# The last up projection by seven block products, with GpSimd forming the weight and token sums

## The chip, the cores and the metric

The kernel runs on one core of a Trainium2 chip. The metric is the device time in microseconds from the first to the last instruction of one execution, as the median of several runs. The core's engines run side by side, each in the order of its own instructions: TensorE (PE in the rows; its weight loads are PEld), VectorE (DVE), ScalarE (ACT), GpSimd (POOL) and the DMA queues (SP's issues most of them here). They meet through semaphores. TensorE's granted clock was 1.00 of full speed (2.4 GHz, the higher of its two levels) over the whole execution before.

## What is computed

The reference runs two transformer-like blocks over 512 tokens of width 1024. What the change touches is the very last feed-forward part, `swiglu` on the normalised and modulated stream `y`:

```python
def swiglu(y, w_in, w_out):
    a, b = jnp.split(y @ w_in, 2, axis=-1)
    return (jax.nn.silu(a) * b) @ w_out
...
D_FF = 2816
...
x = ada_out(x, swiglu(ada_in(x, mod, 2, norm_pre[l, 2]), ffn_w_in[l, 1], ffn_w_out[l, 1]),
            mod, 2, norm_post[l, 2], 0.5)
```

`y @ w_in` is the up projection, 512 x 1024 by 1024 x 5632. Its 5632 columns are 44 tiles of 128; tile j (of `a`) and tile 22 + j (of `b`) make one pair, 22 pairs in all. `@ w_out` is the down projection, 512 x 2816 by 2816 x 1024.

## The kernel before

**Numbers in two parts.** Matmuls take fp32 numbers as a high part (rounded to the matmul's format) and a low part (the rest). `mm3` makes one product of them by three matmuls: high by high, high by low, low by high (lines 540 to 542 in the profile). Activations of 1024 x 512 live in HH and HL (8 blocks of 128 x 512 each), hidden values in GH and GL.

**Weights.** They stream from HBM in chunks of 128 x 1024 fp32 (eight blocks of 128 x 128, so one tile of 128 output columns over the whole depth of 1024). SP issues the loads in order into the ring `stage` of 4 slots; a slot is loaded again once the chunk in it has been split. ScalarE copies a chunk to WH (line 1708) and VectorE subtracts to get WL (line 2569). WH and WL are rings of 3 chunks: a chunk can be split once TensorE has finished the one three before it. TensorE waits for `wlo` of its chunk.

**The last feed-forward part** (`swiglu("y", 1, half, ...)`, half 0 and half 1). Each half does 11 pairs: tile "sa" (8 blocks, 24 matmuls of 512 columns), tile "sb" (24 more), each in a bank of PSUM from a ring of 6. ScalarE applies silu to "sa" (line 2129) into SCR, VectorE multiplies "sb" onto it (line 3182), ScalarE writes the high part to GH (`hidden`, line 1728) and VectorE the low part to GL (`hidden_low`, line 2611). Then eight tiles "sd" of the down projection run over the 11 hidden blocks of this half, and the second half is added. The first pair and "sa" of the second are entwined with the norm ahead of them. GpSimd has nothing to do in this part until the closing norm. X, Z, TAB, CB and MST are tensors in SBUF that earlier stages used; CB and MST (128 x 2 x 1024 each) and TAB (128 x 2048) are idle by then.

**What sets the order.** Every engine's program is written out by hand, in the same loops; `weights(name, ahead)` on ScalarE and VectorE splits the chunks that the named tile needs, and some ahead.

Of the kernel before, what the change touches and what calls it, by code (L numbers as in the profile page):

```python
# [12 lines left out]
S = 512  # L13
# [198 lines left out]
def program(nc, ws, wm, xT, cT, params, cond, consts, max_rows, out, plan):  # L212
# [3 lines left out]
    with ctx:  # L216
# [101 lines left out]
        def hx(k, n=S):  # L318
            return HH[:, k, 0:n], HL[:, k, 0:n]
# [93 lines left out]
        EARLY_GROUPS = [("n2", 0), ("n1", 1), ("n2", 1), ("an", 2, 0)]  # L413

        def operands(i):
            q = early_up(i)
            if q is None:
                return WH[:, i % NW, :], WL[:, i % NW, :]
            a = (12 + 2 * q) * S
            return GHf[:, a:a + 1024], GLf[:, a:a + 1024]  # L420

        def operands_free(i):

            if early_up(i) is not None:
# [91 lines left out]
        def tensor(e):  # L516
# [3 lines left out]
            def block(*specs):  # L520
                if cur["used"] + len(specs) > 8:
                    cur["n"] += 1
                    cur["used"] = 0
                    if dry:
                        chunks.append([])
# [617 lines left out]
            def ending():  # L1143
# [25 lines left out]
                plus(3, 1)  # L1169

            def swiglu(who, f, half, n, mov, ready):
# [509 lines left out]
        def scalar(e):  # L1681
# [3 lines left out]
            def weights(name=None, ahead=AHEAD):  # L1685

                want = -1 if name is None else upto.get(name, -1)
                while at["w"] <= min(want + ahead, len(chunks) - 1):
                    i = at["w"]
                    src, wh, _ = low_stage(i)  # L1690
                    if split_done(i)[0] is wlo and chunks[i][0][0] == "poolm":
# [412 lines left out]
            def closing_norm():  # L2104
# [8 lines left out]
                yield from ada_norm(0, 0, S, hx)  # L2113

            def swiglu(who, f, half, n, zt):
                def hidden(jj):
# [3 lines left out]

                for jj in range(11):
                    pair = jj == 0 and half == 0
# [7 lines left out]
                    if not pair:  # L2130
                        weights(("sb", who, half, jj))
                        walk.tick()
                hidden(10)
                if (who, half) == ("c", 1):
                    walk.pace = (1, 1)
                for nn in range(8):
# [7 lines left out]
                    if who == "y" and half and nn == 7:  # L2144
                        break
                    act.wait_ge(mm, "sd", who, half, nn)
                    if half == 0:
# [391 lines left out]
        def vector(e):  # L2539
# [3 lines left out]
            def weights(name=None, ahead=AHEAD):  # L2543

                want = -1 if name is None else upto.get(name, -1)
                while at["w"] <= min(want + ahead, len(chunks) - 1):
                    i = at["w"]
                    src, wh, wl = low_stage(i)
                    of = folded_weights(i)
# [594 lines left out]
            def closing_norm():  # L3144
# [13 lines left out]
                yield from ada_norm(0, 0, S, xx, hx)  # L3158

            def swiglu(who, f, half, n, zt):  # L3160
                def hidden_low(jj):
# [9 lines left out]

                for jj in range(11):
                    pair = jj == 0 and half == 0
# [7 lines left out]
                    dve.wait_ge(ev, "sa", who, half, jj)  # L3181
                    made(e.tensor_tensor(T, bank("sb", who, half, jj)[:, 0:n], T, ALU.mult), "sb", who, half, jj)  # L3182
                if n == S:
                    hidden_low(10)
# [3 lines left out]
                for nn in range(8):  # L3188
                    step("sd", who, half, nn)
                    if who == "y" and half and nn == 7:  # L3190
                        break
# [455 lines left out]
        def gpsimd(e):  # L3647
# [180 lines left out]
            half_root(k2, 1)  # L3828

            def end_root(s):  # L3830
# [21 lines left out]
        def sync(e):  # L3852
# [9 lines left out]
            def load(i):  # L3862
                if i >= NS:
                    sp.wait_ge(*split_done(i - NS))
# [255 lines left out]
```

## Time and profile before

| | us |
|---|---|
| median of 3 runs | 2936.25 |
| lowest, highest | 2935.87, 2936.34 |
| the profiled execution | 2936.28 |
| its span, first to last instruction | 2934.7 |
| TensorE busy | 2923.9 |
| VectorE busy | 1783.2 |
| ScalarE busy | 1128.4 |
| GpSimd busy | 238.3 |

The profiled execution is 1.6 us longer than its span and 0.03 us from the median. Busy times come from one execution. Matmuls are pipelined, so the distance from one matmul's start to the next, not its duration, says what it costs. An engine's busy time says nothing of the end unless something waits for it.

### The profile page before, as it was taken

Reading aid. Unit: us, or ns where it says so; the run is one execution under the profiler, and the core shown is the slowest. Engines: PE = TensorE matmul, PEld = TensorE weight load, DVE = VectorE, ACT = ScalarE, POOL = GpSimd, SP = SyncE. Lnnn points to the kernel's source line nnn. Section 1 sums busy time; section 2 is a strip of 40 time slices with the busy share of each in tenths; the row PEclk is TensorE's granted clock in tenths of the full one; section 3 lists DMA queues with packets and bytes.
Section 4 is the critical chain, followed back from the end, with each engine's and each line's share of the span. In section 5 each row is a group of like instructions: output and inputs, shape, how many; then the busy total and the mean of one; then the engine's idle time right before and its main releaser. Section 6 shows DMA issues by size and latency. Waiting matters only on the chain.

```text
span 2934.7 us, 36398 instructions
## 1 busy us (share of the span) xinstructions
PE 2923.9 (100%) x14793; PEld 2485.4 (85%) x14793; DVE 1783.2 (61%) x2639; ACT 1128.4 (38%) x1731; POOL 238.3 (8%) x202
## 2 busy tenths in 40 slices
PE   9999999999999999999999999999999999999999
PEld 8988888888888888888888899888889887888887
DVE  7867666865767776778856656332348667542234
ACT  4432333433534333324433345222225457432222
POOL 0300100000001200100000011000002006100001
PEclk9999999999999999999999999999999999999999
DMA  7444455334433432344434435222234340222221
GB/s 306 159 172 149 150 172 186 139 138 141 136 136 115 156 124 100 125 146 138 157 132 148 137 129 173 101 93 101 93 108 173 116 144 30 72 87 100 94 97 69
DMA packets 109334, 384.75 MB, mean 131 GB/s; under 512 B 12136, under 2 KB 15720, under 8 KB 109168
## 3 DMA queue, kind: packets, MB, share of 16 engines
q1 hardware_dynamic: 84528, 295.31, 28.6%
q10 hardware_dynamic: 24640, 87.12, 8.6%
q8 instruction: 117, 1.92, 0.3%
q14 instruction: 49, 0.40, 0.0%
HBM read 380.27 MB, written 2.11 MB: 130 GB/s over the span
## 4 chain that ended last, share of the span: by engine, by line
PE 98%; ACT 1%; POOL 0%; DVE 0%; issue 0%; DMA 0%; POOLq 0%; SPq 0%; DVEq 0%; ACTq 0%
PE ps L540 30%; PE ps L541 30%; PE ps L542 30%; PE ps L755 1%; PE ps L770 1%; PE ps L756 1%; PE ps L669 1%; PE ps L606 0%; PE ps L607 0%; PE ps L610 0%; PE ps L643 0%; POOL GL L3678 0%; DMA X<-xT 0%; PE ps L1373 0%; PE ps L1372 0%
## 5 line engine op out<-in xcount | busy, mean ns | idle before, releaser
L2569 DVE TENSOR_TENSOR WL<-stage,WH 128x1024 fp32r<-128x1024 f32 x496 | 614.0, 1239 | 552.4 <-ACT WH L1708 551.8
L540 PE MATMUL ps<-HH,WH 128*128 128x512 f32 x2152 | 839.7, 390 | 0.1
L541 PE MATMUL ps<-HL,WH 128*128 128x512 f32 x2152 | 836.2, 389 | 0.0
L542 PE MATMUL ps<-HH,WL 128*128 128x512 f32 x2152 | 835.9, 388 | 0.0
L1708 ACT ACTIVATE WH<-stage 128x1024 fp32r<-128x1024 f32 x499 | 524.1, 1053 | 429.6 <-PE ps L542 422.1
L540 PE MATMUL ps<-GH,WH 128*128 128x512 f32 (+2 forms) x1678 | 574.4, 342 | 0.0
L541 PE MATMUL ps<-GL,WH 128*128 128x512 f32 (+2 forms) x1678 | 572.6, 341 | 0.0
L542 PE MATMUL ps<-GH,WL 128*128 128x512 f32 (+2 forms) x1678 | 572.6, 341 | 0.0
L542 PEld LDWEIGHTS ps<-HH,WL 128*128 128x128 f32 x2152 | 404.1, 188 | 84.1
L540 PEld LDWEIGHTS ps<-HH,WH 128*128 128x128 f32 x2152 | 404.3, 188 | 81.9 <-issue 1.1
L541 PEld LDWEIGHTS ps<-HL,WH 128*128 128x128 f32 x2152 | 404.3, 188 | 80.1
L540 PEld LDWEIGHTS ps<-GH,WH 128*128 128x128 f32 x1678 | 317.8, 189 | 38.3
L541 PEld LDWEIGHTS ps<-GL,WH 128*128 128x128 f32 x1678 | 317.9, 189 | 37.6
L542 PEld LDWEIGHTS ps<-GH,WL 128*128 128x128 f32 x1678 | 317.8, 189 | 35.9
L1728 ACT ACTIVATE GH<-SCR 128x512 fp32r<-128x512 f32 (+5 forms) x310 | 165.9, 548 | 420.1 <-DVE SCR L2907 125.2
L2596 DVE CUSTOM_DVE_ANT_0 MST<-MST,CB,PAR 128x1024 f32<-128x1024 f32 x158 | 205.2, 1299 | 2.3 <-DMA MST<-wm 1.8
L2611 DVE TENSOR_TENSOR GL<-SCR,GH 128x512 fp32r<-128x512 f32 (+1 forms) x192 | 124.3, 656 | 58.8 <-ACT GH L1728 57.2
L3678 POOL TENSOR_TENSOR GL<-SCR,GH 128x512 fp32r<-128x512 f32 (+3 forms) x102 | 121.8, 1212 | 412.0 <-ACT GH L1728 411.6
L2026 ACT ACTIVATE SCR<-ps,PAR 128x512 f32<-128x512 f32 x88 | 68.0, 775 | 153.2 <-PE ps L542 138.3
L3182 DVE TENSOR_TENSOR SCR<-ps,SCR 128x512 f32<-128x512 f32 (+1 forms) x66 | 39.7, 602 | 122.1 <-PE ps L542 110.8
L3656 POOL TENSOR_TENSOR V<-V,HM 128x4 f32<-128x4 f32 (+1 forms) x20 | 25.7, 1285 | 1033.2 <-DVE V L2639 1033.2
L2129 ACT ACTIVATE SCR<-ps 128x512 f32<-128x512 f32 (+1 forms) x66 | 34.7, 525 | 185.6 <-PE ps L542 178.8
(333 smaller groups left out, 2920.6 us busy)
## 6 DMA issues: line engine op xcount, KB each, us to landing
stage<-ws SPq DMA_DIRECT2D x533, 512.0 KB, 3.3
MST<-wm ACTq DMA_DIRECT2D x154, 512.0 KB, 3.3
Z<-wm SPq DMA_DIRECT2D x10, 512.0 KB, 8.9
TAB<-consts ACTq DMA_DIRECT2D x7, 448.0 KB, 3.5
MST<-wm SPq DMA_DIRECT2D x6, 512.0 KB, 9.0
Z<-max_rows ACTq DMA_DIRECT2D x8, 256.0 KB, 4.3
out<-X SPq DMA_DIRECT2D x16, 128.0 KB, 1.8
X<-xT SPq DMA_DIRECT2D x2, 512.0 KB, 6.1
```

The lines of the kernel that those rows point to most:

```text
L540: e.matmul(o, wh, mh, start=start, stop=False, **more)
L541: e.matmul(o, wh, ml, start=False, stop=False, **more)
L542: return e.matmul(o, wl, mh, start=False, stop=stop, **more)
L1708: e.activation(wh, src, ACT.Copy).then_inc(whi.sem, whi.up(("w", i)))
L1728: e.activation(dst, src, ACT.Identity if "bias" in more else ACT.Copy, **more).then_inc(hi.sem, hi.up(name))
L2026: e.activation(T, bank("up", l, c)[:, :], ACT.Identity, scale=par("cw", (l * 3 + 1) * 44 + c), bias=par("cb", l * 44 + c)).then_inc(ev.sem ...
L2129: e.activation(T, bank("sa", who, half, jj)[:, 0:n], ACT.Silu).then_inc(ev.sem, ev.up(("sa", who, half, jj)))
L2569: e.tensor_tensor(wl, src, wh.bitcast(F32), ALU.subtract).then_inc(wlo.sem, wlo.up(("w", i)))
L2596: e.tensor_tensor_reduce(out=products, in0=a, in1=b, scale=1.0, scalar=res if i else bias, op0=ALU.mult, op1=ALU.add, accum_out=res).then_inc(
L2611: e.tensor_tensor(dst, src, high_part.bitcast(F32), ALU.subtract).then_inc(lo.sem, lo.up(name))
L3182: made(e.tensor_tensor(T, bank("sb", who, half, jj)[:, 0:n], T, ALU.mult), "sb", who, half, jj)
L3678: e.tensor_tensor(dst, src, high_part.bitcast(F32), ALU.subtract).then_inc(plo.sem, plo.up(name))
```

## The change

Pairs 3 to 10 of half 0 and all 11 of half 1 (19 of 22) are computed in another way. Take the weights of a pair as four blocks, each 512 deep by 128 columns: A11 and A12 are the upper and lower half of the depth of tile "sa", A21 and A22 those of "sb". Take the activations as four blocks too: B11 and B21 (upper and lower half of the depth, tokens 0 to 255), B12 and B22 (tokens 256 to 511). The plain way needs eight block products. The new one (Strassen's scheme in Winograd's form) needs seven:

- weight sums, new for each pair, by GpSimd (`weight_sums_of`): S1 = A21 + A22, S2 = S1 - A11, S3 = A11 - A21, S4 = A12 - S2, each 128 x 512
- token sums, once, by GpSimd ahead of the first such pair: four instructions add HH and HL back to full numbers in Z (128 x 1024 each, `restored`), then T1 = B12 - B11, T2 = B22 - T1, T3 = B22 - B12, T4 = B21 - T2 (128 x 1024 each)
- products A11 B11, A12 B21, S2 T2, S1 T1, S3 T3, A22 T4, S4 B22, each 4 blocks deep: 12 matmuls of 256 columns. They are entwined between pairs: S2, S1, S3 of pair n, A11 of pair n+1, A22 of n, A12 of n+1, S4 of n.

Bank 1 of a pair adds up A11, S2, S3, A22; ScalarE keeps a copy after A11, S2 and S3 in TAB (`keep`, 128 x 256). Bank 2 has A12, bank 3 has S1 and then S4. VectorE adds bank 2 and the first copy (C11), bank 3 and the third (C22, before S4 may go on in that bank), bank 3 and the second (C12); ScalarE's silu runs on C11 and C12 together, and VectorE multiplies by what bank 1 holds in the end and by C22 (`gated`, two instructions).

WH and WL hold half chunks ("units", one for each product): `high_unit` and `low_unit` split one of 128 x 512, six products ahead, since the rings are still 3 chunks. Unit m + 6 follows when product m has ended. A stage slot of such a pair comes free when the units and the GpSimd sums made from it are done. GpSimd makes the sums of a pair in CB or MST by turns, once the unit S4 of the pair two before is split.

```diff
+FAST_FROM = (3, 0)
...
+def fast_order(r):
+
+    last = 10 - FAST_FROM[r]
+    order = [(0, "A11"), (0, "A12")]
+    for n in range(last + 1):
+        order += [(n, "S2"), (n, "S1"), (n, "S3")]
+        order += [(n + 1, "A11")] * (n < last) + [(n, "A22")]
+        order += [(n + 1, "A12")] * (n < last) + [(n, "S4")]
+    return order
...
+        def unit_free(r, n, p):
+
+            v, side = ring_place[r, n, p]
+            return (mm, *ring_user.get((v - NW, side), ring_user[v - NW]))
...
+            def fast_pairs(r):
...
+                for n, p in FAST[r]:
+                    if p == "A11":
+                        P = take_bank(("fast", r, n, 1), dv, "first half", r, n)
+                    elif p == "A12":
+                        P = take_bank(("fast", r, n, 2), dv, "C11", r, n)
+                    elif p == "S1":
+                        P = take_bank(("fast", r, n, 3), dv, "C12", r, n)
+                    else:
+                        P = bank("fast", r, n, 3 if p == "S4" else 1)
+                    wh, wl = unit(r, n, p)
+                    pe.wait_ge(wlo, "u", r, n, p)
...
+                    elif p == "S4":
+                        pe.wait_ge(dv, "C22", r, n)
+                    for k in range(4):
+                        at = slice(k * 128, k * 128 + 128)
+                        inst = mm3(P[:, 0:256], wh[:, at], wl[:, at], *moving(p, k), k == 0 and p in ("A11", "A12", "S1"), k == 3,
+                                   skip_group_check=True)
...
-                for jj in range(11):
+                for jj in range(FAST_FROM[half] if who == "y" else 11):
...
+                if who == "y":
+                    fast_pairs(half)
...
+            def high_unit(r, m):
+
+                n, p = FAST[r][m]
+                act.wait_ge(*unit_free(r, n, p))
+                if p[0] == "S":
+                    act.wait_ge(psum, "S", r, n, int(p[1]))
+                else:
+                    i = fast_chunk[r, n, int(p[1]) - 1]
+                    act.wait_ge(landed[i % NS], "w", i)
+                e.activation(unit(r, n, p)[0], unit_source(r, n, p), ACT.Copy).then_inc(whi.sem, whi.up(("u", r, n, p)))
...
+                if who == "y":
+                    if half == 0:
+                        high_sum(2)
+                        high_sum(3)
+                        high_unit(0, 0)
+                        high_unit(0, 1)
+                        high_sum(4)
+                        high_sum(1)
+                        hidden(FAST_FROM[0] - 1)
+                        for m in range(2, 6):
+                            high_unit(0, m)
...
+            def low_unit(r, m):
+                n, p = FAST[r][m]
+                wh, wl = unit(r, n, p)
+                dve.wait_ge(whi, "u", r, n, p)
+                e.tensor_tensor(wl, unit_source(r, n, p), wh.bitcast(F32), ALU.subtract).then_inc(wlo.sem, wlo.up(("u", r, n, p)))
...
+                for m, (n, p) in enumerate(order):
+                    if p == "S2" and n:
+                        gated(n - 1)
+                    elif p == "S3":
+                        if n:
+                            hidden_low(FAST_FROM[r] + n - 1)
+                        last_block(n)
+                    elif p == "A12":
+                        first_block(n)
+                    elif p == "S4":
+                        second_block(n)
+                    if m + 6 < len(order):
+                        low_unit(r, m + 6)
...
+            pool.wait_ge(lo, "h", k2, 7, 1)
+            for k in range(0, 8, 2):
+                restored(k)
+            pool.wait_ge(psum, "h", 6)
+            token_difference(1, Z[:, 0:4, 256:512], Z[:, 0:4, 0:256])
+            pool.wait_ge(psum, "T", 1)
+            token_difference(2, Z[:, 4:8, 256:512], token_sum(1))
+            token_difference(3, Z[:, 4:8, 256:512], Z[:, 0:4, 256:512])
+            pool.wait_ge(psum, "T", 2)
+            token_difference(4, Z[:, 4:8, 0:256], token_sum(2))
...
+                before = two_before(r, n)
+                if before:
+                    pool.wait_ge(wlo, "u", *before, "S4")
+                    pool.wait_ge(psum, "S", *before, 4)
+                else:
+                    pool.wait_ge(lo, "T", 4 if n else 3)
+                    pool.wait_ge(psum, "T", 4)
...
+                one(1, below[:, 0:512], below[:, 512:1024], ALU.add)
+                pool.wait_ge(psum, "S", r, n, 1)
+                one(2, weight_sum(r, n, 1), above[:, 0:512], ALU.subtract)
+                one(3, above[:, 0:512], below[:, 0:512], ALU.subtract)
+                pool.wait_ge(psum, "S", r, n, 2)
+                one(4, above[:, 512:1024], weight_sum(r, n, 2), ALU.subtract)
...
             def load(i):
-                if i >= NS:
+                if i - NS in fast_chunk:
+                    r, n, part = fast_chunk[i - NS]
+                    sp.wait_ge(wlo, "u", r, n, ("A12", "A22")[part])
+                    sp.wait_ge(psum, "S", r, n, (4, 3)[part])
+                elif i >= NS:
                     sp.wait_ge(*split_done(i - NS))
```

Three places of the engines' programs show it. First VectorE in the middle of half 0. Before, one pair takes two splits of 1024 elements, one product from PSUM and one low part of 512:

```order
L3182 TENSOR_TENSOR SCR<-ps,SCR 128x512 [waits s_ev,s_mm]
L2569 TENSOR_TENSOR WL<-stage,WH 128x1024 [waits s_whi]
L2611 TENSOR_TENSOR GL<-SCR,GH 128x512 [waits s_hi]
L2569 TENSOR_TENSOR WL<-stage,WH 128x1024 [waits s_whi]
L3182 TENSOR_TENSOR SCR<-ps,SCR 128x512 [waits s_ev,s_mm]
```

Now one pair (L3379 is a low unit, L3399 C11, L3407 C12, L3403 C22, L3413 and L3415 the two of `gated`, L2826 `hidden_low`):

```order
L3379 TENSOR_TENSOR WL<-stage,WH 128x512 [waits s_whi]
L3407 TENSOR_TENSOR SCR<-ps,TAB 128x256 [waits s_mm]
L3379 TENSOR_TENSOR WL<-stage,WH 128x512 [waits s_whi]
L3413 TENSOR_TENSOR SCR<-ps,SCR 128x256 [waits s_ev]
L3415 TENSOR_TENSOR SCR<-TAB,SCR 128x256 [waits s_dv]
L3379 TENSOR_TENSOR WL<-MST,WH 128x512 [waits s_whi]
L3379 TENSOR_TENSOR WL<-CB,WH 128x512 [waits s_whi]
L2826 TENSOR_TENSOR GL<-SCR,GH 128x512 [waits s_hi]
L3403 TENSOR_TENSOR TAB<-ps,TAB 128x256 [waits s_ev]
L3379 TENSOR_TENSOR WL<-CB,WH 128x512 [waits s_whi] x2
```

Four instructions for a pair became thirteen (with one more low unit and C11 ahead of this piece), all in one queue, and the first half of `gated` stands behind C12 and one low unit.

Second, GpSimd from the last norm to the end of the kernel. Before, it goes from the norm ahead of the last part straight to the closing norm:

```order
L3806 TENSOR_TENSOR V<-V,HM 128x2 [waits s_mm,s_dv]
L3833 TENSOR_TENSOR V<-V,HM 128x2 [waits s_mm,s_dv]
L3838 TENSOR_TENSOR X<-X,SCR 128x256 [waits s_dv] x3
L3833 TENSOR_TENSOR V<-V,HM 128x2 [waits s_dv]
L3838 TENSOR_TENSOR X<-X,SCR 128x256 [waits s_dv] x5
```

Now eight token instructions and then four weight sums for each of 19 pairs stand between (L4126 `restored`, L4130 the token differences, L4157 the weight sums):

```order
L4101 TENSOR_TENSOR V<-V,HM 128x2 [waits s_mm,s_dv]
L4126 TENSOR_TENSOR Z<-HH,HL 128x1024 [waits s_lo]
L4126 TENSOR_TENSOR Z<-HH,HL 128x1024 x3
L4130 TENSOR_TENSOR TAB<-Z 128x1024 [waits s_psum]
L4130 TENSOR_TENSOR CB<-Z,TAB 128x1024 [waits s_psum]
L4130 TENSOR_TENSOR CB<-Z 128x1024
L4130 TENSOR_TENSOR MST<-Z,CB 128x1024 [waits s_psum]
L4157 TENSOR_TENSOR CB<-stage 128x512 [waits s_lo,s_psum,s_ws2,s_ws1]
L4157 TENSOR_TENSOR CB<-CB,stage 128x512 [waits s_psum]
L4157 TENSOR_TENSOR CB<-stage 128x512
L4157 TENSOR_TENSOR CB<-stage,CB 128x512 [waits s_psum]
```

All read both inputs from SBUF.

Third, VectorE where the fast pairs of half 0 begin (L3459 is the product of pair 2, L2826 with 128x1024 or 4x256 the low part of a token sum):

```order
L3459 TENSOR_TENSOR SCR<-ps,SCR 128x512 [waits s_ev,s_mm]
L2826 TENSOR_TENSOR GL<-CB,GH 128x1024 [waits s_hi] x2
L3379 TENSOR_TENSOR WL<-stage,WH 128x512 [waits s_whi] x2
L2826 TENSOR_TENSOR GL<-MST,GH 128x1024 [waits s_hi]
L2826 TENSOR_TENSOR HL<-TAB,HH 128x4x256 [waits s_hi]
L2826 TENSOR_TENSOR GL<-SCR,GH 128x512 [waits s_hi]
L3379 TENSOR_TENSOR WL<-CB,WH 128x512 [waits s_whi] x3
L3379 TENSOR_TENSOR WL<-stage,WH 128x512 [waits s_whi] x2
```

The units of the first two products stand behind the low parts of T2 and T3, and the third unit (S2) behind those of T4 and T1 and behind pair 2's hidden block.

## Rows read from the trace of the kernel before

**Rows 1.** The page: busy time, share of the span and instructions of each engine.

```profile
PE 2923.9 (100%) x14793; PEld 2485.4 (85%) x14793; DVE 1783.2 (61%) x2639; ACT 1128.4 (38%) x1731; POOL 238.3 (8%) x202
```

**Rows 2.** Stretch: length, busy PE, PEld, DVE, ACT, POOL; clock, DMA share, GB/s.

```profile
2595.20:2682.20 87.00, 87.00 (x386) 72.03 (x385) 29.95 (x32) 24.99 (x32) 0.00 (x0) 1.00 0.28 96
2742.00:2862.00 120.00, 120.00 (x531) 99.39 (x530) 40.03 (x43) 34.33 (x44) 0.00 (x0) 1.00 0.27 97
```

**Rows 3.** Timeline (start us, us, engine, line): matmuls of 512, later 256 columns.

```profile
2585.12 0.39 PE L541 MATMUL ps<-HL,WH 128*128 128x512 f32 x1
...
2587.38 0.39 PE L542 MATMUL ps<-HH,WL 128*128 128x512 f32 x1
...
2226.82 0.28 PE L542 MATMUL ps<-GH,WL 128*128 128x256 f32 x1
...
2227.78 0.28 PE L541 MATMUL ps<-GL,WH 128*128 128x256 f32 x1
```

**Rows 4.** Timeline of VectorE from the norm's last low parts to pair 2's product.

```profile
2572.16 2.06 DVE L2615 SCALAR_TENSOR_TENSOR HL<-SCR,MOD,HH 128x256 fp32r<-128x256 f32 x5
2574.14 1.22 DVE L2569 TENSOR_TENSOR WL<-stage,WH 128x1024 fp32r<-128x1024 f32 x1
2580.75 0.69 DVE L3182 TENSOR_TENSOR SCR<-ps,SCR 128x512 f32<-128x512 f32 x1 [5.38 <-ACT SCR L2129]
2582.14 0.69 DVE L2611 TENSOR_TENSOR GL<-SCR,GH 128x512 fp32r<-128x512 f32 x1 [0.70 <-ACT GH L1728]
2583.57 1.23 DVE L2569 TENSOR_TENSOR WL<-stage,WH 128x1024 fp32r<-128x1024 f32 x1 [0.74 <-ACT WH L1708]
...
2585.50 1.23 DVE L2569 TENSOR_TENSOR WL<-stage,WH 128x1024 fp32r<-128x1024 f32 x1
2586.65 0.68 DVE L2611 TENSOR_TENSOR GL<-SCR,GH 128x512 fp32r<-128x512 f32 x1
...
2595.29 0.69 DVE L3182 TENSOR_TENSOR SCR<-ps,SCR 128x512 f32<-128x512 f32 x1 [2.64 <-PE ps L542]
```

**Rows 5.** Timeline: GpSimd instructions of 256 and 512 elements, VectorE not in their way.

```profile
2253.01 0.74 POOL L3678 TENSOR_TENSOR GL<-SCR,GH 128x256 fp32r<-128x256 f32 x1 [3.23 <-ACT GH L1728]
...
985.82 1.29 POOL L3692 TENSOR_TENSOR SCR<-stage 128x512 f32<-128x512 f32 x1 [5.14 <-DMA stage<-ws]
987.07 1.30 POOL L3693 TENSOR_TENSOR stage<-stage 128x512 f32<-128x512 f32 x1
```

**Rows 6.** Timeline of VectorE after that last GpSimd instruction.

```profile
987.31 1.61 DVE L2558 TENSOR_TENSOR WL<-SCR,WH 128x512 fp32r<-128x512 f32 x1 [1.90 <-ACT WH L1701]
988.84 0.68 DVE L2559 TENSOR_TENSOR WL<-stage,WH 128x512 fp32r<-128x512 f32 x1
989.44 0.41 DVE L2881 TENSOR_TENSOR SCR<-ps,SCR 128x255 f32<-128x255 f32 x1
989.77 0.41 DVE L2882 TENSOR_TENSOR SCR<-ps,SCR 128x255 f32<-128x255 f32 x1
```

**Rows 7.** Timeline of GpSimd and VectorE, both busy, from 98.8 to 103 us.

```profile
99.32 1.90 POOL L3692 TENSOR_TENSOR SCR<-stage 128x512 f32<-128x512 f32 x1 [5.31 <-DMA stage<-ws]
101.17 1.48 POOL L3693 TENSOR_TENSOR stage<-stage 128x512 f32<-128x512 f32 x1
...
98.83 1.23 DVE L2569 TENSOR_TENSOR WL<-stage,WH 128x1024 fp32r<-128x1024 f32 x1 [1.05 <-ACT WH L1708]
99.97 0.61 DVE L2611 TENSOR_TENSOR GL<-ps,GH 128x256 fp32r<-128x256 f32 x2
100.49 2.44 DVE L2611 TENSOR_TENSOR GL<-SCR,GH 128x256 fp32r<-128x256 f32 x2
```

**Rows 8.** Timeline of ScalarE: silu, then the high part of the product.

```profile
2580.05 0.60 ACT L2129 ACTIVATE SCR<-ps 128x512 f32<-128x512 f32 x1
2581.47 0.63 ACT L1728 ACTIVATE GH<-SCR 128x512 fp32r<-128x512 f32 x1 [0.83 <-DVE SCR L3182]
```

**Rows 9.** DMA issues in half 0's changed stretch: count, KB each, median us to landing.

```profile
stage<-ws SPq DMA_DIRECT2D x16, 512.0 KB, 3.2
```

More of the change, by code:

```diff
@@ L24 @@
 POOL_BY_VECTOR = (0, 3, 5)
+FAST_FROM = (3, 0)
[7 more added lines that the diff above has]
+    return order
+FAST = [fast_order(r) for r in range(2)]
 def pool_reach(g, t):
@@ L413, in program, with place_chunk, place_products @@
         EARLY_GROUPS = [("n2", 0), ("n1", 1), ("n2", 1), ("an", 2, 0)]
+        ring_place, ring_user, fast_chunk = {}, {}, {}
+        def place_chunk(i):
+            v = ring_place["next"] = ring_place.get("next", -1) + 1
+            ring_place[i], ring_user[v] = v, ("w", i)
+        def place_products(r, first):
+            v = ring_place["next"] + 1
+            for m, (n, p) in enumerate(FAST[r]):
+                ring_place[r, n, p] = v + m // 2, m % 2
+                ring_user[v + m // 2] = ("prod", r, n, p)
+                ring_user[v + m // 2, m % 2] = ("prod", r, n, p)
+            ring_place["next"] = v + (len(FAST[r]) - 1) // 2
+            for n in range(11 - FAST_FROM[r]):
+                for part in range(2):
+                    fast_chunk[r, n, part] = first + 2 * n + part
+                    fast_chunk[first + 2 * n + part] = r, n, part
@@ new lines, in high_sum, with keep @@
+            def high_sum(q):
+                act.wait_ge(psum, "T", q)
+                if q == 1:
+                    act.wait_ge(mm, "sb", "y", 0, FAST_FROM[0] - 1)
+                high(sum_parts(q)[0], token_sum(q), "T", q)
+            def keep(r, n, q):
+                act.wait_ge(mm, "prod", r, n, ("A11", "S2", "S3")[q - 1])
+                before = two_before(r, n)
+                if before:
+                    act.wait_ge(dv, ("C11", "C12", "second half")[q - 1], *before)
+                elif n == 1:
+                    act.wait_ge(lo, "T", 1)
+                e.activation(kept(r, n, q), bank("fast", r, n, 1)[:, 0:256], ACT.Copy).then_inc(ev.sem, ev.up(("kept", r, n, q)))
@@ L2119, in hidden @@
                     high(GH[:, jj, 0:n], SA("sa", who, half, jj)[:, 0:n], "shid", who, half, jj)
-                for jj in range(11):
+                for jj in range(FAST_FROM[half] if who == "y" else 11):
                     pair = jj == 0 and half == 0
@@ L2145, in swiglu @@
                         break
+                    if (who, half, nn) == ("y", 0, 7):
+                        for m in range(4):
+                            high_unit(1, m)
                     act.wait_ge(mm, "sd", who, half, nn)
@@ L3170, in step @@
                         walk.tick()
-                for jj in range(11):
+                for jj in range(FAST_FROM[half] if who == "y" else 11):
                     pair = jj == 0 and half == 0
@@ L3182, in swiglu @@
                     made(e.tensor_tensor(T, bank("sb", who, half, jj)[:, 0:n], T, ALU.mult), "sb", who, half, jj)
+                if who == "y":
+                    if half == 0:
+                        low_sum(2)
+                        low_sum(3)
+                        low_unit(0, 0)
+                        low_unit(0, 1)
+                        low_sum(4)
+                        low_sum(1)
+                        hidden_low(FAST_FROM[0] - 1)
+                        for m in range(2, 6):
+                            low_unit(0, m)
+                    else:
+                        low_unit(1, 4)
+                        low_unit(1, 5)
+                    fast_pairs(half, hidden_low)
                 if n == S:
@@ L3189, in swiglu @@
                     step("sd", who, half, nn)
+                    if (who, half, nn) == ("y", 0, 7):
+                        for m in range(4):
+                            low_unit(1, m)
                     if who == "y" and half and nn == 7:
```

158 lines of the change are left out of this document (152 added, 6 removed).

## The prediction

> **What bounds the kernel now.** Read first the busy times: TensorE is busy for 2923.9 of 2934.7 us, all else far less [rows 1]. In the two stretches that change it is busy for all 87.0 and all 120.0 us, at a granted clock of 1.00, while VectorE works 30 and 40 us there and GpSimd nothing [rows 2]. So this part lasts as long as its matmuls, and what counts is the distance between their starts. Of 512 columns: ten starts lie 2.26 us apart, 0.2267 each (the sum of a tile of 24 goes by that); of 256 columns, in an earlier stage: eight starts 0.96 apart, 0.120 each [rows 3]. A product (12 matmuls of 256) is 1.44 us. Half the columns cost more than half the time, so seven products for eight gain less than an eighth.
>
> **What TensorE gains.** A pair took 48 x 0.2267 = 10.88 us and takes 7 x 1.44 = 10.08: 0.80 less, and 19 pairs 15.2 less. That is all there is to win; nothing else on TensorE goes away. From 2936.3 (the profiled execution; the median is the same) this would be 2921.1.
>
> **What the others get for one pair.** ScalarE: seven splits of 512, three copies of 256, silu and a high part. Instructions of 512 take 0.60 to 0.63 [rows 8], so with all twelve at that it is 7.5 of 10.08; it isn't the bound. DMA: 1 MB per pair as before, 3.2 us to landing [rows 9], 0.28 of the engines' time [rows 2]; hidden. VectorE: instructions of 512 follow each other in 0.60 (988.84 to 989.44), of 256 in 0.33 to 0.34 [rows 6], of 1024 in 1.14 (98.83 to 99.97) [rows 7]. Seven low units and one hidden low part are 8 x 0.60, five of 256 are 1.7: 6.5 us. GpSimd: a sum of 512 takes 1.25 from start to start, four are 5.0; one of 1024 is 1.29 + 2 x 0.55 = 2.4 by the step from 256 to 512 [rows 5]. Each of these alone fits in 10.08.
>
> **They don't fit together.** While GpSimd runs to 988.37 (alone, in 1.30), VectorE's subtraction of two SBUF tensors that begins at 987.31 takes 1.61 for 0.69: it stands still until GpSimd has ended, then does its work [rows 5, 6]. From 98.83 both have a queue. GpSimd's instruction of 99.32 takes 1.90: it waits for VectorE's end at 99.97 and needs 1.25 from there. Two of VectorE's with one input in PSUM (99.97) run meanwhile at full speed, 0.61 for both. Its next two, both inputs in SBUF, take 2.44 for 0.6: one runs when GpSimd's first has ended, then GpSimd's second (1.48 for 1.29), then the other [rows 7]. So: an instruction of VectorE with two inputs in SBUF and one of GpSimd exclude each other for their whole length, they take turns when both wait, and one with an input in PSUM is free. The Trainium skill, "SBUF — State Buffer", on the shared port, says so too: an exclusive lock, and two SBUF inputs contend with a GpSimd instruction that reads SBUF; the trace agrees with its 1.61 us. The page doesn't say who comes next; by it alone the four free ones could all hide and a cycle would be 10.1 us, by the turns of rows 7 it is more.
>
> Of VectorE's work per pair the low units, the hidden low part (8 x 0.60) and the second of `gated` (0.34, TAB and SCR) exclude GpSimd: 5.14 us. With GpSimd's 5.0 that is 10.14, already over 10.08. The four with PSUM (1.36) are free, but VectorE runs in order, so they hide only if one stands next while GpSimd works. I drew a cycle, with turns: GpSimd has work in 7.4 us of it, C22 and C11 hide, C12 and the first of `gated` don't (+0.68), and VectorE waits 0.13 for silu behind C12 (a follow-up on ScalarE begins 0.03 after, 0.63 long [rows 4, 8], beside one low unit of 0.60). So **10.95 to 11.0 us** a cycle where GpSimd works, against 10.08 of TensorE, and 10.88 before.
>
> **Where TensorE feels it.** VectorE may fall behind. Units are six ahead, 7.2 us, less 1.35 for the split itself. Tighter is bank 1: A11 of pair n + 1 takes the bank that the first of `gated` of pair n - 1 reads. When TensorE sets the pace, that one ends 1.6 us into the cycle, and A11 may start at 4.3. So 2.6 us of lag are free, then TensorE waits 0.9 per cycle.
>
> **Half 0, the beginning.** GpSimd may start when the norm's last low part is done, 2574.2; VectorE's split takes the turn (to 2575.3) [rows 4]. Then 2.4 each: three `restored` to 2582.5, VectorE 0.6, the fourth to 2585.5, VectorE 1.14 (its split of 2583.57), T1 to 2589.05, VectorE 0.6, T2 2592.05, T3 2594.45, T4 2596.85. (The split of 2585.50 is of a later chunk and falls away.) TensorE ends pair 2 at 2595.1 [rows 4]. VectorE: low parts of T2 and T3 2596.85 to 2599.15, unit 0 to 2599.75. So A11 starts at 2599.85, **4.7 us late**. GpSimd's S1 to 2601.0, unit 1 2601.6, S2 2602.9, low T4 2604.05, S3 2605.3, low T1 2606.45, S4 2607.7, hidden 2608.3, next pair's S1 2609.55, unit 2 (S2) **2610.15**, and with one sum of the next pair between each: unit 3 2612.0, unit 4 2613.9, unit 5 2615.75. TensorE has done A11 and A12 by 2603.15 and waits 7.1; products 3, 4, 5 wait 0.4 each. It ends product 5 at 2617.3 for 2595.1 + 6 x 1.44 = 2603.8: **13.5 us lost**. Bound below: had VectorE gone first each time, unit 2 would be 3.7 earlier: 9.8. Bound above: 1024 elements at twice 1.30, +0.2 x 8: 15.
>
> **Half 0, the rest.** GpSimd's sums for pair 2 need a slot of `stage` (unit 6 at 2616.35, 3.2 us of load): they start at 2619.8, and those of pair 3 follow at once when unit S4 of pair 1 is split (2627.8). The lag is used up there: by the hand-drawn turns A11 of pairs 2 to 7 starts at 2626.0, 2638.3, 2649.3, 2660.3, 2671.3, 2682.3; then nine products, end 2695.3. Unhindered from 2617.3 it were 50 x 1.44 later, 2689.3: **6.0 lost**. The eight pairs end 13.1 us later than they did (2682.2).
>
> **Half 1.** Sums of its first two pairs are made during the down projection, whose last products hide them. Nine cycles are loaded. Lag grows by 1.3 in the first (no `gated`, no hidden yet), then 0.9 each; the fourth waits 0.7, six more 0.92 each: **6.2 lost** for 8.8 won. Behind each half the last hidden block is done some 3.3 us after the last product (C12, silu, two of `gated`, high, low), and the down projection needs it after ten blocks, 30 x 0.2267 = 6.8: hidden, cost nothing; without that cover 3 us each.
>
> **Sum:** 2936.3 - 15.2 + 13.5 + 6.0 + 6.2 = **2946.8, say 2947**. Half 0 loses 13, half 1 wins 2.6.
>
> **Rivals.**
> 1. It works as drawn: VectorE and GpSimd find gaps, the cycle stays at 10.08 and the token sums are nearly done in time. For it: VectorE's own 6.5 us leave 3.6 free, and all four PSUM instructions could hide; the lag is forgiven at first. Against: rows 7, and 10.14 of excluding work. Time: 2921.1 + 3 for a beginning in which pair 0's S2 is 3 late, 2924. It decides by whether excluding work per cycle is under 10.08. Chance 0.17.
> 2. Turns cost less: VectorE, with its next instruction ready, gets the port again before GpSimd. Beginning 9.8, cycle 10.4 (half of the free ones hide more): about 2 and 3 lost later. 2921.1 + 9.8 + 5 = 2936, no change. Chance 0.2.
> 3. Chained sums are dearer: S2 waits for S1 and S4 for S2 by a semaphore, and every sum meets a low unit; if each handover takes 0.1 more, a cycle is 11.8. Fifteen loaded cycles, thirteen past the free lag: +0.8 each, 10. 2957. Chance 0.13.
> My forecast: 0.5.
>
> **How the numbers follow.** About 0.2% (5.9 us) is what a measurement of this kernel can tell from no change. Slower takes the forecast and rival 3: 0.63. Same is rival 2: 0.20. Faster is rival 1: 0.17. The range 2927 to 2958 leaves out most of rival 1 and the tail of rival 3, together under 0.2; inside are the bounds of the beginning (9.8 to 15) and of the cycle (10.4 to 11.8).
>
> **What would show it.** In the trace after: 256-column starts 0.120 apart within a product; a gap before the first A11 (4 to 5 us) and a larger one before the first S2 (about 7), both ended by WL or low parts of VectorE; low units of 0.69 alone, but near 1.9 where GpSimd works; GpSimd's sums between 1.3 and 1.9; A11 of consecutive pairs 11.0 apart in the middle of both halves, 10.1 at their ends, waits before A11 ended by the first of `gated`. Half 1 from its first product to its last near 117 us. I am wrong if VectorE's low units stay at 0.7 beside GpSimd, if the waits are on ScalarE or DMA, or if A11 is 10.1 apart throughout.

## The result, and the profile after

| | before | after |
|---|---|---|
| median of 12 runs, us | 2936.19 (2935.75 to 2936.99) | 2943.15 (2942.14 to 2943.53) |
| profiled execution, span, us | 2934.7 | 2941.2 |
| ratio after to before | | 1.0023, 95% from 1.0015 to 1.0031 |

The changed kernel is slower by 7 us, 0.23%, for 2947 forecast. The spans differ by 6.5; everything below is reckoned in those. The page of after, busy times:

```profile
PE 2916.0 (99%) x15477; PEld 2509.9 (85%) x15477; DVE 1910.7 (65%) x2814; ACT 1190.5 (40%) x1887; POOL 382.4 (13%) x286
```

TensorE is busy 7.9 us less than before [rows 1], and the span is 6.5 longer: what was won went into waits, and a part of the busy time is matmuls at a lower clock (below). Two windows of after, half 0 from the last plain product's end to the first block of the down projection, and half 1's up projection (columns: stretch, length, busy PE, PEld, DVE, ACT, POOL; clock, DMA share, GB/s). Fast pairs are counted from 0 in each half below, as in the code; "pair 2" at the beginning of half 0 is the last plain one:

```profile
2594.70:2692.40 97.70, 86.25 (x674) 84.79 (x674) 91.08 (x108) 52.37 (x99) 53.52 (x33) 0.95 0.29 92
2752.20:2867.70 115.50, 112.95 (x926) 111.35 (x926) 102.60 (x137) 67.34 (x129) 57.83 (x36) 1.00 0.30 101
```

VectorE is busy 91 of 98 us, where it was 30 of 87 [rows 2]. Half 0 lasts 97.75 from start to start, for 8 x 10.88 = 87.0 before: 10.7 worse. Half 1 lasts 115.4 for 11 x 10.88 = 119.7: 4.2 better. The sum is the 6.5.

**The beginning of half 0.** TensorE, VectorE and GpSimd of after, each its timeline (start us, us, engine, line; then, in brackets, the idle time before it and who ended it):

```profile
2594.38 0.39 PE L632 MATMUL ps<-HH,WL 128*128 128x512 f32 x1
2598.52 0.35 PE L630 MATMUL ps<-HH,WH 128*128 128x256 f32 x1 [3.75 <-DVE WL L3379]
...
2600.27 0.41 PE L631 MATMUL ps<-HL,WH 128*128 128x256 f32 x1
2600.49 0.41 PE L632 MATMUL ps<-HH,WL 128*128 128x256 f32 x1
...
2607.90 0.58 PE L630 MATMUL ps<-GH,WH 128*128 128x256 f32 x1 [4.79 <-DVE WL L3379]
...
2615.89 0.28 PE L630 MATMUL ps<-GH,WH 128*128 128x256 f32 x1
```

```profile
2594.81 0.69 DVE L3459 TENSOR_TENSOR SCR<-ps,SCR 128x512 f32<-128x512 f32 x1 [6.25 <-PE ps L632]
2595.42 2.35 DVE L2826 TENSOR_TENSOR GL<-CB,GH 128x1024 fp32r<-128x1024 f32 x2
2597.68 2.38 DVE L3379 TENSOR_TENSOR WL<-stage,WH 128x512 fp32r<-128x512 f32 x2
2599.98 2.29 DVE L2826 TENSOR_TENSOR GL<-MST,GH 128x1024 fp32r<-128x1024 f32 x1
2602.20 2.29 DVE L2826 TENSOR_TENSOR HL<-TAB,HH 128x1024 fp32r<-128x1024 f32 x1
2604.42 1.75 DVE L2826 TENSOR_TENSOR GL<-SCR,GH 128x512 fp32r<-128x512 f32 x1
2606.10 5.12 DVE L3379 TENSOR_TENSOR WL<-CB,WH 128x512 fp32r<-128x512 f32 x3
2611.14 2.38 DVE L3379 TENSOR_TENSOR WL<-stage,WH 128x512 fp32r<-128x512 f32 x2
```

```profile
2593.14 2.40 POOL L4130 TENSOR_TENSOR MST<-Z,CB 128x1024 f32<-128x1024 f32 x1
2598.00 1.51 POOL L4157 TENSOR_TENSOR CB<-stage 128x512 f32<-128x512 f32 x1 [2.47 <-DVE GL L2826]
2599.59 1.61 POOL L4157 TENSOR_TENSOR CB<-CB,stage 128x512 f32<-128x512 f32 x1
```

Pair 2 ends at 2594.6 (last start, 2594.38, and a matmul's pitch). A11 starts at 2598.52, 3.9 later, S2 at 2607.90 instead of 2.88 behind A11, which is 6.5 more, and the four products from there (S2, S1, S3 and A11 of fast pair 1) are two slow and two fast until the last of them ends at 2615.89: 7.99 for 4 x 1.44, 2.2 more. Together **12.6** (3.91, 6.50 and 2.23).

Who is late? GpSimd's last token sum ends at 2595.5. Before that VectorE sat idle for 6.25 us; low parts 2 and 3 stand behind pair 2's product in its program and begin when it has ended (2595.42). The first units follow (2597.68), and GpSimd idles 2.47 us until the low part of sum 3 frees CB. So the first stop is an **order on VectorE**, no lack of time on either engine. The second stop is **turns**: from 2599.98 each of VectorE's instructions takes 1.1 longer than it needs (2.29 for some 1.2), because a weight sum goes first, and S2's unit is the fourth in that row.

Third, the **clock**: in the second stretch below (2598.50 on) it is 0.59 of 2.4 GHz, a mean of both levels; where it is low, starts are 0.213 apart (2600.27 to 2600.49, rounded) instead of 0.120. Windows of after, TensorE alone:

```profile
2594.70:2598.50 3.80, 0.07 (x1) 1.00 0.00 0
2598.50:2602.70 4.20, 4.18 (x22) 0.59 0.00 0
2602.70:2608.00 5.30, 0.51 (x5) 0.81 0.20 66
2608.00:2611.00 3.00, 3.00 (x14) 0.50 0.14 57
2611.00:2614.00 3.00, 3.00 (x21) 0.70 0.00 0
```

Slow A11 and A12 cost nothing: S2 waits for VectorE anyhow. Slow S2 and S1 do. An estimate from these rows: VectorE has S3's unit ready at 2611.2 (2606.10 plus 5.12) and that of pair 1's A11 at about 2612.9 (the first of the two at 2611.14), so at full clock this A11 would have begun at 2613.0 and ended at 2614.4 instead of 2615.89: about 1.5 of the 12.6.

**The middle.** From fast pair 3 of half 0 on a cycle is 10.54 us (2645.49 to 2656.03, 2666.57 and 2677.11). TensorE of after; the second row stands for four like it, the last is of the half's last pair:

```profile
2634.95 0.35 PE L630 MATMUL ps<-GH,WH 128*128 128x256 f32 x1 [1.04 <-ACT TAB L2276]
...
2656.03 0.36 PE L630 MATMUL ps<-GH,WH 128*128 128x256 f32 x1 [0.23 <-ACT TAB L2276]
...
2689.42 0.36 PE L630 MATMUL ps<-GH,WH 128*128 128x256 f32 x1 [0.56 <-ACT TAB L2276]
```

A start normally 0.12 behind comes 0.51 behind: 0.39 lost. It is S3 that waits, for ScalarE's copy behind S2 (`keep 2`, L2276). Why that is late, ScalarE and then VectorE and GpSimd of after in the same cycle:

```profile
2654.99 0.63 ACT L2287 ACTIVATE SCR<-SCR 128x512 f32<-128x512 f32 x1 [1.39 <-DVE SCR L3407]
2655.52 0.36 ACT L2276 ACTIVATE TAB<-ps 128x256 f32<-128x256 f32 x1
```

```profile
2648.14 3.07 DVE L3379 TENSOR_TENSOR WL<-CB,WH 128x512 fp32r<-128x512 f32 x2
2651.14 1.77 DVE L3379 TENSOR_TENSOR WL<-stage,WH 128x512 fp32r<-128x512 f32 x1
2652.83 0.41 DVE L3399 TENSOR_TENSOR SCR<-ps,TAB 128x256 f32<-128x256 f32 x1
2653.17 1.45 DVE L3379 TENSOR_TENSOR WL<-stage,WH 128x512 fp32r<-128x512 f32 x1
2654.54 0.41 DVE L3407 TENSOR_TENSOR SCR<-ps,TAB 128x256 f32<-128x256 f32 x1
```

```profile
2647.58 1.38 POOL L4157 TENSOR_TENSOR MST<-stage 128x512 f32<-128x512 f32 x1 [4.04 <-DMA stage<-ws]
2649.03 1.63 POOL L4157 TENSOR_TENSOR MST<-MST,stage 128x512 f32<-128x512 f32 x1
2650.63 1.74 POOL L4157 TENSOR_TENSOR MST<-stage 128x512 f32<-128x512 f32 x1
2652.32 1.75 POOL L4157 TENSOR_TENSOR MST<-stage,MST 128x512 f32<-128x512 f32 x1
```

Read from the end: the copy (2655.52) stands behind the silu (2654.99), this waits 1.39 for C12 (L3407, 2654.54), and C12 stands behind units of 1.77 and 1.45 us that would take 0.69, because GpSimd's four sums are among them.

**The last pair of each half.** 2689.42 and 2864.73: A22 stands right behind S3 with no next pair's A11 between them, and waits for the copy of S3: 0.72 and 0.75.

### The profile page after: what moved, and what is told of

The parts are those of the page before. It is cut to its first block, busy times and chain, and to the rows that moved or that the text cites. A ratio compares the mean times of both kernels' runs of the same rounds, so it can differ in the third digit from the quotient of the medians.

```text
span 2941.2 us, 38310 instructions
## 1 busy us (share of the span) xinstructions
PE 2916.0 (99%) x15477; PEld 2509.9 (85%) x15477; DVE 1910.7 (65%) x2814; ACT 1190.5 (40%) x1887; POOL 382.4 (13%) x286
## 4 chain that ended last, share of the span: by engine, by line
PE 96%; DVE 2%; ACT 1%; issue 1%; POOL 0%; POOLq 0%; DVEq 0%; ACTq 0%
PE ps L630 30%; PE ps L631 29%; PE ps L632 29%; DVE WL L3379 1%; PE ps L845 1%; PE ps L860 1%; PE ps L846 1%; PE ps L759 1%; PE ps L724 1%; PE ps L696 0%; PE ps L697 0%; PE ps L700 0%; PE ps L733 0%; POOL GL L3973 0%; PE ps L1506 0%
## 5 line engine op out<-in xcount | busy, mean ns | idle before, releaser
L2784 DVE TENSOR_TENSOR WL<-stage,WH 128x1024 fp32r<-128x1024 f32 x458 | 569.0, 1244 | 449.8 <-ACT WH L1844 449.2
L630 PE MATMUL ps<-HH,WH 128*128 128x512 f32 (+1 forms) x2152 | 808.6, 376 | 3.9 <-DVE WL L3379 3.7
L631 PE MATMUL ps<-HL,WH 128*128 128x512 f32 (+1 forms) x2152 | 805.0, 374 | 0.0
L632 PE MATMUL ps<-HH,WL 128*128 128x512 f32 (+1 forms) x2152 | 804.6, 374 | 0.0
L630 PE MATMUL ps<-GH,WH 128*128 128x512 f32 (+2 forms) x1906 | 640.6, 336 | 10.3 <-ACT TAB L2276 5.5
L631 PE MATMUL ps<-GL,WH 128*128 128x512 f32 (+2 forms) x1906 | 637.5, 334 | 0.0
L632 PE MATMUL ps<-GH,WL 128*128 128x512 f32 (+2 forms) x1906 | 637.5, 334 | 0.0
L631 PEld LDWEIGHTS ps<-GL,WH 128*128 128x128 f32 x1906 | 362.1, 190 | 37.4
L632 PEld LDWEIGHTS ps<-GH,WL 128*128 128x128 f32 x1906 | 362.0, 190 | 36.1
L2826 DVE TENSOR_TENSOR GL<-SCR,GH 128x512 fp32r<-128x512 f32 (+1 forms) x192 | 127.5, 672 | 59.6 <-ACT GH L1864 58.0
L3254 DVE SCALAR_TENSOR_TENSOR SCR<-ps,PAR,SCR 128x511 f32<-128x511 f32 x88 | 65.9, 749 | 62.2 <-ACT SCR L2162 62.2
```

The source lines that it names most:

```text
L630: e.matmul(o, wh, mh, start=start, stop=False, **more)
L631: e.matmul(o, wh, ml, start=False, stop=False, **more)
L632: return e.matmul(o, wl, mh, start=False, stop=stop, **more)
L2784: e.tensor_tensor(wl, src, wh.bitcast(F32), ALU.subtract).then_inc(wlo.sem, wlo.up(("w", i)))
L2826: e.tensor_tensor(dst, src, high_part.bitcast(F32), ALU.subtract).then_inc(lo.sem, lo.up(name))
L3254: made(e.scalar_tensor_tensor(out=T[:, 1:S], in0=p[:, 0:S - 1], scalar=par("cw", (l * 3) * 44 + c), in1=T[:, 1:S], op0=ALU.mult, op1=ALU.a ...
```

## The experiments

Times are medians; the kernel before stands at 2935.9 (the first four) and 2936.1 (the last four).

| run | us | ratio to before, 95% |
|---|---|---|
| small weight sums | 2928.21 | 0.9974 (0.9963 to 0.9984) |
| fills for weight sums | 2928.2, one run | |
| copy before silu | 2939.22 | 1.001 (1.000 to 1.002) |
| two more plain pairs | 2942.63 | 1.0023 (1.0014 to 1.0032) |
| splits in the plain pair | 2934.61 | 0.9995 (0.9986 to 1.0004) |
| both repairs | 2930.35 | 0.9981 (0.9972 to 0.9989) |
| second half only | 2932.57 | 0.9988 (0.9979 to 0.9997) |
| no sums on GpSimd | 2928.63 | 0.9975 (0.9965 to 0.9984) |

**Small weight sums.** All waits and signals stay; beside this edit there is only a fill of half of MST ahead of GpSimd's token work.

```diff
-e.tensor_tensor(weight_sum(r, n, q), a, b, op)
+e.tensor_tensor(weight_sum(r, n, q)[:, 0:16], a[:, 0:16], b[:, 0:16], op)
```

> GpSimd's four weight sums per pair cover 16 of 512 columns (the rest of their tensors keeps what was there, so the output is not the reference's); a fill of half of MST stands ahead of them. All waits and all other instructions stay. Theory A, exclusion: VectorE's instructions with two SBUF inputs and GpSimd's sums take turns, and this makes VectorE's queue 10.5 us per pair. Then low units fall to 0.7 us everywhere, pairs come 10.08 apart, no wait ahead of S3 in the middle of the halves, and the wait before the first S2 falls from 4.8 to about 1.1; total 2931. Theory B, order on ScalarE: the copy after S2 stands behind silu, which stands behind C12; this alone gives the 10.54. Then pairs stay 10.54 apart and only the beginning gains: 2938.

2928.2, 14.9 less than the changed kernel and 2.8 less than theory A said, which left 1.1 of the second stop. One window of it (columns as above), and TensorE's first stop:

```profile
2640.00:2660.00 20.00, 20.00 (x169) 20.00 (x168) 14.64 (x26) 12.41 (x25) 3.52 (x8) 1.00 0.33 106
```

```profile
2598.61 0.42 PE L630 MATMUL ps<-HH,WH 128*128 128x256 f32 x1 [3.75 <-DVE WL L3379]
```

The same window of after has VectorE at 19.58 and TensorE at 19.53. All waits in the middle are gone, and so is the second stop; so both are made by GpSimd's weight sums. The first stop is there as before, 3.75, and so are the last pairs' waits (0.84 and 0.87 from start to start): neither has to do with the sums. Of the 12.6 us of the beginning 5.5 are left, 3.9 of the stop and 1.6 of 17 starts at the lower clock.

**Fills for weight sums.** GpSimd writes the same places for about half as long, but reads nothing.

```diff
-e.tensor_tensor(weight_sum(r, n, q), a, b, op)
+e.memset(weight_sum(r, n, q), 0.5)
```

> GpSimd's weight sums are replaced by fills of the same 128 x 512 (no SBUF input; the output is not the reference's). Theory A in its narrow form (the exclusion needs GpSimd to read SBUF): low units at 0.7 though GpSimd is busy, pairs 10.08 apart, total 2931 to 2933. In a broad form (any GpSimd instruction excludes VectorE's two-input ones): low units are still stretched by the length of a fill, total between 2933 and 2943. Theory B: 2938 or more, pairs 10.54 apart.

2928.2. The low units of this run, by form (duration in ns, least, median, most), and then GpSimd's fills:

```profile
L3379 DVE TENSOR_TENSOR WL<-stage,WH x57: 680/692/694, 2598.0 to 2843.4; 128x512 fp32r<-128x512 f32 x57
L3379 DVE TENSOR_TENSOR WL<-CB,WH x40: 683/693/694, 2602.1 to 2844.8; 128x512 fp32r<-128x512 f32 x40
```

```profile
L4157 POOL MEMSET CB<- 128x512 f32 x40 | 19.9, 526 | 133.5 <-DMA stage<-ws 130.5 <-DVE GL L2826 2.5
```

and the first of these of after:

```profile
L3379 DVE TENSOR_TENSOR WL<-stage,WH x57: 674/1447/1793, 2597.7 to 2857.6; 128x512 fp32r<-128x512 f32 x57
```

Of 133 units none is longer than 0.694 beside 76 fills, where half of the first kind had taken 1.45 and more. 28 of the 133 run beside a fill for over 0.1 us (the one of 2602.10 beside the whole fill of 2602.11). What VectorE and GpSimd exclude each other from is reading. The Trainium skill, "SBUF — State Buffer", on the shared port, states it so, two SBUF inputs only against a GpSimd instruction that reads SBUF; this run agrees. The fills are shorter than the sums, so a share of the 14.9 us may be their length, but a single exclusion would have shown in the longest unit. The time is that of one execution; the reading rests on its trace.

**Copy before silu.** The order on ScalarE in `fast_pairs`; all is computed.

```diff
 elif p == "S2":
+    keep(r, n, 2)
     if n:
         gate(n - 1)
-    keep(r, n, 2)
```

> On ScalarE the copy after S2 comes before the silu of the pair ahead instead of behind it. Theory B: the wait before S3 (0.39 us in each cycle) goes, pairs are 10.08 apart, total 2943 - 13 x 0.4 = 2937 to 2938. Theory A: VectorE's queue is still 10.5 per pair, so the wait only moves, to A11 (first half of the gate) or another place; pairs stay 10.4 to 10.6 apart, total 2942 to 2944.

2939.22, 3.9 less, between what the two theories said. TensorE of this run in the middle:

```profile
2655.89 0.39 PE L630 MATMUL ps<-HH,WH 128*128 128x256 f32 x1
...
2839.67 0.39 PE L630 MATMUL ps<-HH,WH 128*128 128x256 f32 x1 [0.28 <-DVE SCR L3413]
```

The first start is A11 and lies 0.34 behind the one ahead of it; S3 no longer waits. The second is A11 too, in half 1, its wait long enough for the row to name who ended it: L3413, the first of `gated`. The pitch of cycles fell from 10.54 to 10.4. So the chain through silu was what ended the wait, and VectorE's load stands right behind it: the wait moves to A11 by bank 1, where the prediction had put it. In half 1 nothing waits before 2818.6, where the changed kernel waits from 2778.5 on. Each half is 2.0 us shorter than in the changed kernel (95.7 for 97.75 and 113.45 for 115.4).

**Two more plain pairs.** `FAST_FROM = (5, 0)`: five plain pairs in half 0, 17 by seven products. All is computed.

> Five plain pairs ahead in half 0 instead of three. Theory A1: the beginning loses 12.6 us because GpSimd's token sums come too late; with 21.8 us more for them the loss goes: 2943 - 12 + 2 x 0.3 = 2932. Theory A2: it loses them because VectorE does the low parts of T2 and T3 only behind the product of the last plain pair, and GpSimd's weight sums wait for those: the loss moves along unchanged, 2943 + 2 x 0.34 = 2944.

2942.63, 1.4 under what theory A2 said. GpSimd's token sums are done some 20 us ahead now (2597.5, for low parts that begin at 2617.1); TensorE's stops are there all the same:

```profile
2620.22 0.55 PE L630 MATMUL ps<-HH,WH 128*128 128x256 f32 x1 [3.75 <-DVE WL L3379]
...
2629.60 0.50 PE L630 MATMUL ps<-GH,WH 128*128 128x256 f32 x1 [3.92 <-DVE WL L3379]
```

The first is the same to the hundredth. The second is 0.9 shorter only because A11 and A12 ran wholly at the lower clock: S2 starts 9.38 behind A11, exactly as in the changed kernel. It isn't that the token sums are late.

**Splits in the plain pair.** `FAST_FROM = (4, 0)`, and the splits of sums 2 to 4 and of units 0 to 3 are inside the last plain pair; the hidden part of that pair goes to where later ones have theirs. VectorE's part of it (ScalarE's is alike, ahead of its silu and behind its `weights`):

```diff
     T = SA("sa", who, half, jj)[:, 0:n]
+    if who == "y" and half == 0 and jj == FAST_FROM[0] - 1:
+        low_sum(2)
+        low_sum(3)
+        low_sum(4)
+        for m in range(4):
+            low_unit(0, m)
     dve.wait_ge(mm, "sb", who, half, jj)
```

> The whole computation is done. 18 tile pairs by seven products instead of 19, and the splits of the token sums 2 to 4 and of the first four units stand inside the last plain pair on ScalarE and VectorE instead of behind it. Theory A2 (the 12.6 us of the beginning are lost because VectorE makes the low parts of the token sums and of the first units only behind the last plain pair's product, and GpSimd's first weight sums wait for the low part of sum 3): TensorE stops less than 1 us at the beginning, and its clock stays at 2.4 GHz there. Sum: before 2935.9, less 18 x 0.80 = 14.4, plus 4.5 (middle of half 0 as in the changed kernel), plus 4.6 (half 1), plus at most 1 at the beginning: 2931 to 2932. Theory T (turns of VectorE and GpSimd at the start cost it, wherever the splits stand): the beginning still loses 7 to 12, 2938 to 2943.

2934.61. TensorE of this run, the three longest stops:

```profile
2610.96 0.36 PE L630 MATMUL ps<-HH,WH 128*128 128x256 f32 x1 [0.69 <-DVE HL L2830]
...
2626.09 0.36 PE L630 MATMUL ps<-GH,WH 128*128 128x256 f32 x1 [2.42 <-ACT TAB L2276]
...
2637.39 0.36 PE L630 MATMUL ps<-GH,WH 128*128 128x256 f32 x1 [0.99 <-ACT TAB L2276]
```

The beginning loses 0.85 in the first of them (the start 0.97 behind the last) and 0.4 in two smaller waits instead of 12.6, and the clock is 1.00 throughout. The order theory holds; the theory that turns cost it wherever the splits stand does not. My sum missed by 2.6 to 3.6: pair 1's S3 now waits 2.42 where the changed kernel waited 0.37. Eight weight sums and VectorE's units run in turns from 2600.9 to 2615.4, and VectorE stands idle for 0.15 us in all from 2596.8 to 2626.9: its lag, which the long stop used to swallow, is now seen two cycles on. All in all the fast pairs of half 0 last 78.5 us for 49 products of 1.44, 7.9 more than their matmuls, where they lasted 17.1 more in the changed kernel; the turns are still paid for in part.

**Both repairs.** The run above with the copy ahead of the silu as well.

> The whole computation is done. As the run with the splits in the last plain pair, and with ScalarE's copy behind S2 ahead of the silu of the pair before. If the two causes are independent, it saves what the copy alone saved, 4: 2927 to 2928, ratio 0.997, which is faster than both kernels. If the copy's gain had come out of waits that the late beginning had set up, it gives 2931, the same as without it.

2930.35, 4.3 less than without the copy, for 3.9 when it was made alone: the two causes are independent. It missed the forecast by 2.4 to 3.4, as the run above did. This kernel computes all, and it is **faster than both kernels**, by 5.7 and 12.8 us. It has 18 fast pairs, as the run above. The 5.7 is 0.19%, from 0.11% to 0.28%: clear of no change, though small. Its longest stop, A11 of pair 2 waiting for the first of `gated` (L3417):

```profile
2626.59 0.39 PE L630 MATMUL ps<-HH,WH 128*128 128x256 f32 x1 [1.64 <-DVE SCR L3417]
```

**Second half only.** Half 0 is the kernel before, all eleven pairs of half 1 go by seven products (`FAST = [[], fast_order(1)]` and `FAST_FROM = (11, 0)`); all is computed.

> The whole computation is done. Only the eleven pairs of half 1 go by seven products; half 0 is the kernel before, and half 1 needs the token sums, which GpSimd and VectorE have made long ahead. By the terms as the changed kernel showed them: 11 x 0.80 = 8.8 won, 4.6 lost in the middle and at the last pair: 2931.7. If half 0's late start had also pushed work onto half 1, or if the token sums' cost only moves to this place, 2936 or more.

2932.57 for 2931.7. The waits are those of after's half 1 (0.51 or 0.52 from start to start before each S3, 0.44 before the first that waits, 0.87 at the last pair), and the half lasts 115.8 us, 3.9 less than plain; by the medians 3.5 are won. Half 1's gain stands by itself; the loss of the change is all in half 0.

**No sums on GpSimd.** The weight sums as in the first run, and the token sums over 8 and 4 columns of each tile (16 elements of 1024 in each instruction), with fills for the rest.

> Leaves out nearly all of both kinds of sums: the weight sums are taken over 16 of 512 columns and the token sums over 16 columns of each tile, the rest is filled with constants. The splits stay where the changed kernel has them. Theory A2 (order on VectorE): the first stop of TensorE before A11 stays at about 4.1 us, the time is that of the run with small weight sums alone, 2928. Theory T (GpSimd's token sums are late or disturb VectorE there): the first stop shrinks to under 2, 2925 or less.

2928.63, as with small weight sums alone, and the first stop is there:

```profile
2599.24 0.55 PE L630 MATMUL ps<-HH,WH 128*128 128x256 f32 x1 [3.75 <-DVE WL L3379]
```

GpSimd's token sums cost nothing; the 3.75 is what VectorE does ahead of A11: pair 2's product, two low parts and the first unit (2594.81 to 2598.37 in the changed kernel).

## Why the prediction was right, and where not

**TensorE's gain, 19 x 0.80 = 15.2: held.** Starts within a product are 0.120 apart at full clock. With the sums made small, 15.2 less the first stop (3.9), 17 starts at the lower clock behind it (1.6) and the last pairs (1.5) leave 8.2; the spans differ by 8.5.

**The lock and the turns: held in kind.** Low units of 0.69 alone, 1.45 to 1.78 beside sums; with fills or small sums none. The size was too large: where each meets a unit the third and fourth sum start 1.6 and 1.7 behind the one ahead (2649.03, 2650.63, 2652.32), with a unit of 0.6 between them, so one holds the port some 1.0 to 1.1, not the 1.25 that I took from [rows 5]. A cycle cost 0.46 above 10.08, half of the 0.9 that I had. How much of the missing 0.4 to 0.45 is the shorter hold, and how much is that the sums come in one block behind the load (GpSimd waits 4.04 for `stage` at 2647.58), so that VectorE's PSUM instructions fall otherwise than I had drawn, no run here separates.

**Where TensorE feels it: wrong.** I named bank 1 and a free lag of 2.6 us, and waits on ScalarE as a sign that I was wrong. The first place that gives way is S3, by way of low unit, C12, silu, copy, so the wait in the middle is on ScalarE: that sign came true, although what makes the copy late is VectorE's stretched queue. I had the silu's wait on C12 in the drawn cycle (0.13 for VectorE) and did not look at what stands behind the silu on ScalarE. When this chain was cut, the bank was next and 10.4 the pitch, so it was second by some 0.1 us a cycle.

**The beginning: 12.6 by 2615.9 for 13.5; the number was near, the reasons were not quite.** My first term was a late token sum 4 (2596.85), and A11 4.7 late. It was done by 2595.5 and A11 was 3.9 late, for a reason that the program's order shows: `low_sum(2)` stands behind pair 2's product. I had read that as GpSimd's pace and missed that the order alone gives 3.9, which no faster GpSimd mends (last run) and a move of the splits does. S2's start I had at 2610.15 and it was 2607.90; the turns there were real. What made up a part of the difference, about 1.5 us by the estimate above, was the clock, which is in no step of the prediction. A beginning that came 0.8 and then 2.3 us sooner than drawn and then ran at the lower clock gives 12.6 for 13.5 partly by luck; and this term decides the sign, since without it the other terms leave the kernel some 6 us faster (15.2 less 4.5 and 4.55).

**The rest of half 0: 4.5 for 6.0; half 1: 4.55 for 6.2, 115.4 us for 117.** Both by the pitch. (The 6.2 was itself a little high: 1.3 and eight times 0.9 of lag, less the free 2.6, are 5.9 for the nine cycles that the prediction counts.) In them is a term that I called hidden: the tails cost nothing in the down projection, as I said, but inside the last pair of each half A22 waits 0.7 for the copy of S3. The schedule's `(n < last)` shows that nothing stands between S3 and A22 there.

**Sum.** 2936.3 - 15.2 + 12.6 + 4.5 + 4.55 = 2942.75; measured 2943.15. The forecast of 2947 was 3.9 high: 0.9 at the beginning, 1.5 and 1.65 in the rest of the halves, less the 0.4 that the terms leave unexplained. The range, 2927 to 2958, was wide enough to hold no change too, so what the result bears out is the sign and the larger terms, not the range. Of the rivals, the cheaper turns were nearer on the pitch (10.4, for 10.54 measured) and wrong on the beginning (9.8); "as drawn" fell with VectorE's units at 1.45 to 1.78; dearer chained sums too, since the second sum in a chain (1.63 at 2649.03) takes no longer than those behind it, and a cycle is 10.54, not 11.8.

## What to carry to other kernels

When work is moved to an idle engine that shares a port with a busy one, add up the excluding work of both and compare it with the cycle of the engine that sets the pace, but then follow each engine's program past the stretched instruction: the wait shows first where a third engine has something urgent queued behind something that waits. Preparation for a new kind of step belongs inside the last old step, since an engine that runs in order makes it late however early its inputs are there. Here those two reorderings, with one pair fewer done the new way (18 for 19), turned 0.23% slower into 0.19% faster, and all is computed.

## What the runs showed of the hardware that I had not expected

- After the stop of 4.1 us from start to start TensorE's granted clock fell to its lower level, 1.2 GHz: the first matmuls still 0.12 apart, then 0.213 from 2599.20 to 2602.41, then 0.12 again; and once more behind the stop of 5.1, from 2607.9 to 2612.7 (0.50 from 2608 to 2611). It was so in every run with a stop of 4.1 (small sums: 0.53 from 2598.6 to 2602.2). Behind stops of 1.9 and 2.7 us, in the two runs with the splits in the plain pair, it stayed at 1.00. Here it cost about 1.5 us on top of the stops, by the estimate above.
- GpSimd's writing beside VectorE's reading costs VectorE nothing: 133 units at 0.69 beside 76 fills, 28 of them while a fill ran.
- With small sums, a sum of 16 columns on GpSimd takes 0.22, but 0.45 to 0.78 when it meets a low unit or a hidden low part of VectorE (0.71 at 2647.19, beside the unit from 2647.12 to 2647.82), and 1.20 beside a low part of 1024: it waits for that one's end, so in this direction too the lock is for a whole instruction.
